# An encoder layer on one core: reordered u, scan, chunk and attention stages, and the out stage's squares added on VectorE

## The reference

```
y_na  = neighbourhood_attention(q, k, v, rpb) @ w_proj_na
y_ssm = (gelu(s5(u)) * sigmoid(gelu(s5(u)) @ w_glu)) @ w_proj_ssm
h = h + (sigmoid(g_na) * y_na + sigmoid(g_ssm) * y_ssm) @ w_out
hn = rms_norm(h, norm2_g)                    # rsqrt(mean(h * h)) per token
h = h + (gelu(conv3(hn @ w_a)) * (hn @ w_g)) @ w_down
out = rms_norm(h, final_g)[:, 16:]
```

## Time and profile before

| | |
|---|---|
| median of three runs | 1544.02 us (1542.68 to 1545.41) |
| profiled execution | 1545.01 us |
| its span, granted TensorE clock | 1543.3 us, 0.984 of full speed |
| busy share: PE, DVE, ACT, POOL | 96%, 37%, 45%, 67% |
| moved by DMA | 277.09 MB, 180 GB/s on average |
| chain that ended last | PE 78%, DVE 10%, ACT 3% |

### The profile page before, as it was taken

How to read it: one execution, slowest core, us unless ns; L and a number is a source line. 1 busy time by engine, 2 the same in 40 slices (tenths; PEclk the granted TensorE clock), 3 DMA queues, 4 the chain that set the end, 5 groups by cost and what they waited for, 6 DMA issues and landing times.

```text
span 1543.3 us, 31379 instructions
## 1 busy us (share of the span) xinstructions
PE 1477.8 (96%) x11825; PEld 1400.3 (91%) x11825; DVE 564.4 (37%) x1140; ACT 692.5 (45%) x916; POOL 1038.8 (67%) x490
## 2 busy tenths in 40 slices
PE   6898898899989999999999999999999999999998
PEld 5898898898879999999999999999999998888886
DVE  3474688887636323442222222222222222003002
ACT  4544443232145445444454554555554554334434
POOL 3400005775368857888778888888888888888885
PEclk9899999999989999999999999999999999999999
DMA  7797544554457645575555556556555556565553
GB/s 231 223 199 195 159 148 150 170 173 130 126 168 225 199 135 164 178 238 187 164 164 183 185 177 190 178 177 190 180 178 187 186 177 207 178 189 189 185 188 134
DMA packets 251258, 277.09 MB, mean 180 GB/s; under 512 B 30748, under 2 KB 237948, under 8 KB 250540
## 3 DMA queue, kind: packets, MB, share of 16 engines
q1 hardware_dynamic: 224864, 250.58, 53.6%
q10 hardware_dynamic: 26252, 25.35, 5.4%
q0 software_dynamic: 64, 0.07, 0.0%
HBM read 263.32 MB, written 12.39 MB: 179 GB/s over the span
## 4 chain that ended last, share of the span: by engine, by line
PE 78%; DVE 10%; ACT 3%; issue 2%; DVEq 2%; ACTq 2%; SPq 1%; DMA 1%; POOL 0%
PE ps L1476 19%; PE ps L1478 19%; PE ps L1477 19%; PE ps L1819 5%; PE ps L1818 5%; PE ps L1820 5%; DVE ps L1010 3%; DVE scan_states L1200 2%; DVEq L1199 1%; PE ps L1676 1%; ACT w_hi L458 1%; DVE w_lo L462 1%; ACTq L750 1%; DMA w_raw<-in_w_in 1%; SPq L409 1%
## 5 line engine op out<-in xcount | busy, mean ns | idle before, releaser
L462 POOL TENSOR_TENSOR w_lo<-w_raw,w_hi 128x1024 fp32r<-128x1024 f32 x420 | 1008.6, 2413 | 466.9 <-ACT w_hi L458 298.9
L458 ACT ACTIVATE w_hi<-w_raw 128x1024 fp32r<-128x1024 f32 x464 | 488.8, 1059 | 741.9 <-PE ps L1478 509.1
L1476 PE MATMUL ps<-act_hi,w_hi 128*128 128x258 f32 (+2 forms) x2432 | 701.4, 288 | 29.6 <-POOL w_lo L462 23.1
L1478 PE MATMUL ps<-act_hi,w_lo 128*128 128x258 f32 (+2 forms) x2432 | 695.4, 286 | 0.0
L1477 PE MATMUL ps<-act_lo,w_hi 128*128 128x258 f32 (+2 forms) x2432 | 694.2, 285 | 0.0
L1476 PEld LDWEIGHTS ps<-act_hi,w_hi 128*128 128x128 f32 x2432 | 466.7, 192 | 36.7 <-issue 18.1
L1477 PEld LDWEIGHTS ps<-act_lo,w_hi 128*128 128x128 f32 x2432 | 467.5, 192 | 0.0
L1478 PEld LDWEIGHTS ps<-act_hi,w_lo 128*128 128x128 f32 x2432 | 465.5, 191 | 0.0
L1818 PE MATMUL ps<-w_hi,hidden_hi 128*128 128x512 f32 x352 | 139.2, 395 | 0.0
L1819 PE MATMUL ps<-w_hi,hidden_lo 128*128 128x512 f32 x352 | 139.0, 395 | 0.0
L1820 PE MATMUL ps<-w_lo,hidden_hi 128*128 128x512 f32 x352 | 139.0, 395 | 0.0
(11 more groups left out here) (251 smaller groups left out, 1563.9 us busy)
## 6 DMA issues: line engine op xcount, KB each, us to landing
w_raw<-in_w_up SPq DMA_DIRECT2D x176, 512.0 KB, 3.5
w_raw<-in_w_in SPq DMA_DIRECT2D x128, 512.0 KB, 4.3
w_raw<-in_w_down SPq DMA_DIRECT2D x88, 512.0 KB, 4.0
w_raw<-in_w_out SPq DMA_DIRECT2D x32, 512.0 KB, 3.5
w_raw<-in_w_proj_na SPq DMA_DIRECT2D x16, 512.0 KB, 3.4
w_raw<-in_w_proj_ssm SPq DMA_DIRECT2D x16, 512.0 KB, 3.5
bias_rows<-skew_scratch ACTq DMA_DIRECT2D x32, 128.0 KB
w_raw<-in_w_glu SPq DMA_DIRECT2D x8, 512.0 KB, 3.5
```

The costliest lines, as they stand in the source:

```text
L458: act.activation(slot(whi, k), slot(raw, k), ACT.Copy).then_inc(s_hi, 1)
L462: pool.tensor_tensor(slot(wlo, k), slot(raw, k), slot(whi, k).bitcast(F), ALU.subtract).then_inc(s_lo, 1)
L1476: mm(o, slot(whi, k)[:, cols], xh[:, kt, lo:lo + n], start=kt == 0, stop=False)
L1478: ins = mm(o, slot(wlo, k)[:, cols], xh[:, kt, lo:lo + n], start=False, stop=kt == units * UKT - 1)
```

## The change

Joined in one edit:

- **Start.** 12 idle matmuls (ones by ones) on TensorE before the first transposes and two before the first product; x tiles go over four PSUM banks instead of three and six ahead instead of four; hi units and token squares lie among the tiles; GpSimd makes the lo parts of units 0 to 11, formerly 0 to 7. `x_feature_major` moves to memory that the b tables use later, so the wait for the spill moves from VectorE's u block to ScalarE's `table_copies`. The spill itself is issued after the root. b is loaded and transposed ahead of c; c is loaded as it lies and paired by a copy on GpSimd. Three small transposes put the query scale on partitions.
- **V and K.** Two V stage buffers. Skew stores: 24 beside K, 16 beside Q, 24 beside the first gate units.
- **Scan.** Unbroken on VectorE. ScalarE copies Q and the six gate blocks unscaled (`q_copy`, `gate_copy`); the query scale is applied in the attention scores (two instructions for one), the gate's by VectorE in attention blocks 2 to 7. GpSimd, not VectorE, makes lo of unit 51. `g_make(1)` moves behind the scan, and each later one is made two steps ahead, formerly three.
- **Chunk loop.** TensorE's order is turned round as the diff shows; the gate block's evacuation comes at t = 2 and 6. The meta scores move into attention block 0. `bias_reach(0)` on GpSimd is one unit later.
- **Queues.** y stores and loads, and the bias and attention loads of blocks 0 and 1, go from ScalarE's queue to SP's, between unit loads.
- **Out stage.** VectorE adds the squares of each tile into PSUM bank 7 (`square_add`), two adds a block, the last into SBUF; one matmul by ones stands after the second unit of the up product, and the root on ScalarE after that half-block's four hi units.

```diff
...
-        vst = at("v_stage", 29696, [P, 4, CB])
+        vst = (at("v_stage_a", 29696, [P, 4, CB]), at("v_stage_b", 25600, [P, 4, CB]))
...
-        x0T = at("x_feature_major", o_y, [P, KT, L])
+        x0T = at("x_feature_major", 52736, [P, KT, L])
...
-        cnat = at("c_rows", 95744, [P, GROUP, 2, STATE])
+        cnat = at("c_rows", 99840, [P, GROUP, 2, STATE])
+        craw = at("c_loaded", o_y + 8704, [P, 2, GROUP, STATE])
...
+            sp.wait_ge(s_crp, 1)
...
+            def skew(c):
+                sp.dma_start(skew_d[c, :, :], pad_d[:, GRID_W - 1 - c:2 * GRID_W - 1 - c]).then_inc(s_pad3, 16)
...
+            for u in range(16):
+                load_in(U_K, HALF, u // 8, (u % 8,))
+                for c in range(3 * u // 2, 3 * (u + 1) // 2):
+                    skew(c)
+            for u in range(16):
+                load_in(U_Q, 0, u // 8, (u % 8,))
+                skew(24 + u)
...
+            def y_store(t):
+                sp.wait_ge(s_yge, t + 1)
+                for b in range(PB):
+                    for g in range(2):
+                        sp.dma_start(y_d[t, b, g, :, :, :].rearrange("c j n -> j c n"),
+                                     U2[64 * g:64 * g + 64, PB * t + b, :]).then_inc(s_yst[t % 2], 16)
...
+            for u in range(24):
+                load_in(U_G, 4 * HALF, u // 8, (u % 8,))
+                skew(40 + u)
+            load_in(U_G, 4 * HALF, 3)
+            for t in range(KH):
+                load_in(U_G, 4 * HALF, 4, (t,))
+                y_store(t)
+                if t:
+                    y_load(t - 1)
+                if t == 5:
+                    sp.wait_ge(s_pad3, 16 * GRID_W)
+                    for n in range(2):
+                        sp.wait_ge(s_kst[n], 16 * 8)
+                        sp.wait_ge(s_vst[n], 16 * 4)
+                    sp.wait_ge(s_gm, KH)
+                    bias_load(sp, 0)
+                    att_load(sp, 0)
+                elif t == 6:
+                    bias_load(sp, 1)
+                    att_load(sp, 1)
+            load_in(U_G, 4 * HALF, 5, range(2))
+            y_load(KH - 1)
...
-            for k in range(2 * DEPTH):
+            for k in range(3 * DEPTH):
...
+            pool.wait_ge(s_cl, 32)
+            pool.tensor_copy(cnat[:, :, :, :].rearrange("p c r n -> p r c n"), craw[:, :, :, :]).then_inc(s_crp, 1)
+
+            pool.wait_ge(s_lo, U_Q + DEPTH - 1)
+            lo_unit(pool, U_Q, DEPTH - 1)
...
+            unit_behind = {0: 0, 4: 1, 8: 2, 9: 3, 11: 4, 13: 5}
...
+                if k == 7:
+                    act.wait_ge(s_const, 2)
+                    token_square(0, 0, 1)
+                    token_square(1, 0, 2)
+                if k in unit_behind:
+                    hi_unit(act, U_U, unit_behind[k])
+            hi_unit(act, U_U, 6)
+            token_square(2, 0, 3)
+            token_square(0, 1, 4)
+            token_square(1, 1, 5)
+            hi_unit(act, U_U, 7)
+            token_square(2, 1, 6)
...
+            act.dma_start(xT_d, x0T[:, :, :].rearrange("p k t -> p (k t)")).then_inc(s_spill, 16)
...
+            def q_copy(n):
+                act.wait_ge(s_used, U_Q + 4 * (n + 1))
...
+            def gate_copy(n):
+                act.wait_ge(s_used, U_G + 4 * (n + 1))
+                banks = 2 * ((n + 1) % 2)
+                act.activation(gate_na[:, 2 * n:2 * n + 2, :], ps[:, banks:banks + 2, 0:NL], ACT.Copy).then_inc(s_ga, 1)
...
+                        if tile >= 2:
+                            act.wait_ge(s_sqa, tile - 1)
...
+                    if first and k == 0:
+                        norm_root(1, NL)
...
+            for c in range(NCH - 1):
+                scan_step(c)
+            dve.nop().then_inc(s_scan, 1)
...
-            g_make(2)
+            g_make(1)
...
-                if t % 4 == 3:
-                    dve.wait_ge(s_used, U_G + 4 * G_SCAN + t + 1)
-                    gate_block(gate_na, 2 * (G_SCAN + t // 4), 0)
+                if t % 4 == 2:
+                    dve.wait_ge(s_used, U_G + 4 * G_SCAN + t + 2)
+                    gate_block(gate_na, 2 * (G_SCAN + t // 4), three_and_one if t == 2 else ps[:, 0:2, 0:NL])
...
-                if t + GSLOTS < KH:
-                    g_make(t + GSLOTS)
+                if t + 2 < KH:
+                    g_make(t + 2)
...
+                for t in range(2):
+                    dve.scalar_tensor_tensor(out=S[:, t:4:2, :], in0=ps[:, 0:2, WK * t:WK * (t + 1)], scalar=qsc[:, t:t + 1],
+                                             in1=bm[:, t:4:2, :], op0=ALU.mult, op1=ALU.add)
...
+                if b >= G_ATT - G_SCAN:
+                    n = b - (G_ATT - G_SCAN)
+                    dve.tensor_tensor(gate_na[:, 2 * n:2 * n + 2, :], gate_na[:, 2 * n:2 * n + 2, :],
+                                      rstd[:, LIVE:L].unsqueeze(1).to_broadcast([P, 2, NL]), ALU.mult).then_inc(s_gsc, 1)
...
+            def square_add(tile):
+                dve.wait_ge(s_sq, tile + 1)
+                if tile == 0:
+                    dve.tensor_copy(ps[:, 7, 0:NL], sq[:, 0, 0:NL]).then_inc(s_sqa, 1)
+                else:
+                    dve.tensor_tensor(sqj[:, 0:NL] if tile == KT - 1 else ps[:, 7, 0:NL], ps[:, 7, 0:NL],
+                                      sq[:, tile % 2, 0:NL], ALU.add).then_inc(s_sqa, 1)
+                dve.drain()
...
+                    for m in range(2):
+                        square_add(4 * i + (2 * k + m))
...
+                    if between and q == 1:
+                        between()
...
+            def idle_passes(n):
+                for _ in range(n):
+                    mm(ps[:, 3, 0:P], ones[:, :], ones[:, :], start=True, stop=True)
+
+            pe.wait_ge(s_const, 1)
+            idle_passes(12)
...
-                b = 4 + k % 3
+                b = 4 + k % 4
...
-            for k in range(4):
+            for k in range(6):
                 x_transposes(k)
...
+                    if q == 0 and m == 1:
+                        x_transposes(6)
+                        x_transposes(7)
+                    if q in (1, 2):
                         x_transposes(4 * q + 4 + 2 * m)
                         x_transposes(4 * q + 5 + 2 * m)
...
+                elif n:
+                    pe.wait_ge(s_qev, n - 1)
...
+                    pe.wait_ge(s_ga, n - 1)
...
+            def gate_half(t, m):
+                half_unit(U_G + 4 * G_SCAN, t, t % 4, 4, m, hnh, hnl, LIVE, NL, ((3, 0)[t // 4], 1)[m])
+
+            pe.wait_ge(s_ga, G_SCAN - 1)
             kernels(0)
-            pe.wait_ge(s_scan, 1)
+            gate_half(0, 0)
+            pe.wait_ge(s_ga, G_SCAN)
+            gate_half(0, 1)
             for t in range(KH):
-                if t == 4:
-                    pe.wait_ge(s_g, G_SCAN + 1 + SEED)
-                half_unit(U_G + 4 * G_SCAN, t, t % 4, 4, 0, hnh, hnl, LIVE, NL, 0)
+                if t + 1 < KH:
+                    gate_half(t + 1, 0)
+                if t == 0:
+                    pe.wait_ge(s_scan, 1)
+                chunk_out(t)
                 if t + 1 < KH:
                     kernels(t + 1)
-                chunk_out(t)
-                half_unit(U_G + 4 * G_SCAN, t, t % 4, 4, 1, hnh, hnl, LIVE, NL, 1)
-            pe.wait_ge(s_g, G_SCAN + G_SSM + SEED)
+                    if t == 3:
+                        pe.wait_ge(s_g, 1 + SEED)
...
                     elif n == 0:
+                        meta_scores()
+                        pe.wait_ge(s_g, G_SSM + SEED)
                         scores(b)
...
+            def norm_sum():
+                pe.wait_ge(s_sqa, KT)
+                mm(ps[:, 6, 0:NL], ones[:, :], sqj[:, 0:NL], start=True, stop=True).then_inc(s_ss, 1)
...
```

More of the change, by code:

```diff
@@ L44 @@
 PAIRS = GROUPS // 2
-SCAN_STEPS = 8
 GSLOTS = 3
@@ L265, in encoder_block @@
         s_vcp = sem("v_copied")
-        s_vst = sem("v_stored")
+        s_vst = [sem(f"v_stored_{i}") for i in range(2)]
         s_wm = sem("w_made")
@@ L427, in _ @@
+            load_in(U_G, 4 * HALF, 5, range(2))
+            y_load(KH - 1)
+            load_in(U_G, 4 * HALF, 5, range(2, 8))
+            with sp.Fori(6, 8) as i:
                 load_in(U_G, 4 * HALF, i)
@@ L722, in _ @@
             hi_unit(act, U_K + DEPTH, 1)
-            act.wait_ge(s_vst, 16 * 8)
+            for n in range(2):
+                act.wait_ge(s_vst[n], 16 * 4)
             act.wait_ge(s_pd, 1)
@@ L1370, in h1_lo @@
                     op0=ALU.mult, op1=ALU.subtract).then_inc(s_nl, 1)
-            with dve.Fori(0, 4) as i:
+            def square_add(tile):
[6 more added lines that the diff above has]
+                dve.drain()
+            for i in range(4):
                 for k in range(2):
@@ L1488, in product @@
                         half_unit(base_u, k0 + q, q, units, m, xh, xl, lo, n, banks[m])
-            def norm_sum(t, first, last, ring, k, n):
-                pe.wait_ge(s_sq, t)
```

(9 more changed lines are left out.)

363 lines of the change are left out of this document (160 added, 203 removed).

## The result

The changed kernel takes 1500.94 us, the median of four runs (1500.06 to 1502.59), against 1543.35 for the kernel before on the same chip: ratio 0.9721, 95% interval 0.9706 to 0.9735. A second comparison on another occasion gave 1499.15 and 0.9708 (0.9689 to 0.9727). The profiled execution's span is 1498.8, 44.5 less than 1543.3.

What follows compares the result with a forecast made beforehand. TensorE, busy 1477.8 of 1543.3 us, was taken as the bound. The terms -14.0 - 11 - 20.7 + 2 - 10.9 - 8.0 gave -62.6; 1545.0 - 62.6 - 1.0 = 1481.4 us, range 1473 to 1500.

Steps and rivals of the forecast that it cites:

- C: Q and six gate blocks: -20.7 us, with the unbroken scan hidden by 3 us and TensorE's own 114.9 of work the bound.
- F: Out stage and up product: -8.0 us, from dropping the norm_sum pairs after blocks for one sum; late root hidden.
- B: From V to K: -11 us, by removing TensorE's waits for w_tr (4.1) and key blocks (3.6); about 1.5 idle stays.
- A: Start and u product: -14.0 us, with the third u block starting at 47.9 instead of 61.90.
- D: Chunk loop: +2 us, as VectorE's work per step stands level with TensorE's; bounds -1.6 and +14.7.
- The lock: Chunk loop, VectorE and GpSimd sharing ports: each shared VectorE operation meets a GpSimd pass, 14.7 us, time 1496; chance 0.12.
- the gate block: Chunk loop at t = 2 and 6: a gate block of 1.2 to 2.3 us comes on top for VectorE.
- E: Start of attention, blocks 0 and 1: -10.9 us, to 28.7, with stores and loads moved to SP; bounds -5 and -13.
- The rival of the queue: SP's queue in the chunk loop: loads stand behind y_store, each step 20.5 instead of 7.1 us, time 1588; chance 0.02.

## Why the prediction was wrong

- **C, right.** 115.12 for 114.9: the unbroken scan lies under TensorE's products, which run without a gap at clock 1.00.
- **F, right**: -9.4 and 0.3 back in the trace, 7.6 alone; 8.0 forecast. A pair of sums cost 0.83 (12.43 for 11.60 a block), where the step took 0.68. The late root cost nothing that shows.
- **B, right within 1.4.** -9.6 for -11. The wait for w_tr, 1.4, is what was forecast as residue; a clock of 0.93 from 129.19 to 155.00 came on top. The second profile of the changed kernel has -11.1, so the 1.4 is within what single executions differ by.
- **A, mis-sized by 3.2.** The first product came at 14.27, as forecast. The first block took 20.7, where the step put 18.7 and the kernel before took 20.8. Neither of the step's two reasons holds. That "one transpose pair fewer is left in it" is not so: both kernels have five pairs inside the block, because in the kernel before the sixth stood ahead of the first product. That "the idle passes end its cold start" gains nothing against the kernel before: in both the first half unit takes 2.86 (here at clock 0.50, 14.27 to 18.00) and the others 1.5 to 1.6. What the passes do is keep the earlier start from having three slow ones. The other 1.1 is in the second block and behind it, where TensorE stands 1.0 at the small transposes; by the code it waits there for VectorE's rows, which the step had not counted.
- **D, right in kind, 1.3 short.** The lock and the gate block were named; the lock was priced for the additions only, and the c products were blocked as well.
- **E, the step that failed, 8.6 us.** It costed the moved y stores by one question, whether weight loads stay two units ahead for TensorE. They did: in this stage TensorE waits for no lo part. What the step left out, as if at no cost, is what else stands behind 4.3 to 11 us of y store issues on SyncE's queue: block 1's bias rows and operands, then the weight unit for ScalarE, whose hi pass waited 10.3 us with the exponentials and block 2's operand issues behind it. The slow clock after each stall (2.74 and 2.04 for half units of 1.5) came on top. Moving block 1's loads alone passed the wait on to the next late thing; leaving most of the stores out took most of it away, and late stores ended it. That shows the stores' place as the cause. How much of it is late issue and how much slow landing behind them (9.7 and 11.9 us) is not parted. And not all of the 8.6 is theirs: with late stores and full clock the stage still takes 30.1, where the step put 28.7, mainly because its block 0 takes 15.9 for 13.7. The rival of the queue looked in the right place for the wrong victim, and at 13.4 us a step for the wrong size.
- **Not in the sum at all: 4.9 us in attention blocks 2 to 7.** The rescale was named as exposed to the lock and given neither a place nor a price. It stood at the one point of the block where TensorE waits for VectorE, with 6.9 to 8.4 us of idle time just ahead of it in four of the six blocks. The early placement gave all of it back.

These misses are 3.2 + 1.3 + 8.6 + 4.9 = 18.0 of the 18.1 between forecast and trace (62.6 and 44.5); what is left in B, C and F and the 1.1 of V about cancel. Range: the sum put each part near its good end, and the low chance for a common loss in E left the top at 1500.

## What to carry to other kernels

When DMA issues move to another queue, count the issue time in front of every later item of that queue, not of the weights alone, look how long each then takes to land, and then look at which engine's in-order work waits for the late one: a ring that keeps TensorE fed may still starve the engine that prepares it. When work is added to an engine with idle time, its place in the engine's order is its price: ahead of a long wait it was free here, behind it, it lay on the path. When a cure moves a stall without shortening the whole, look for a common cause further up the queue, as here.

## What the runs showed of the hardware

The view of the granted clock doesn't tell of this kernel's start. Without idle passes the trace has no record of the clock before 27.07, and the view prints full speed there,

```profile
8.00:14.27 6.27, 5.09 (x19) 2.84 (x19) 3.87 (x10) 4.18 (x9) 2.35 (x1) 1.00 1.10 280
14.25:26.27 12.02, 11.91 (x49) 10.37 (x49) 4.00 (x10) 7.46 (x13) 4.07 (x2) 1.00 0.68 203
```

while half units take 2.85 to 2.89 us as late as 26, nearly twice the 1.5 to 1.6 of later ones. With idle passes there are records from 4.43 on, the row reads 0.50 and the first half unit takes 2.86 as well. At the start the time from one matmul to the next is to be read, not the clock of the row.

The transfer engines stood at a share of 0.27 with 90 GB/s from 402 to 408 while a weight unit took 11.9 us to land, against 4.1 as the median of its kind. So a low mean share was no sign of room there. The y stores are not its only source: with seven of eight pieces left out, slices from 389 to 392 still read 0.27 to 0.28. With y in rows over 128 partitions the same 6 us read 0.55, and the weight unit landed in 11.3. Which transfers filled the engines, and how many of the 16 worked, no view here shows.
